# Twenty-four expert blocks computed ahead of the loop instead of sixteen, a loop period of eight steps, and the final sum joined to the last step

## The chip, the cores and the metric

The kernel runs on one core of one Trainium2 chip. The metric is the device time of one execution in microseconds (us), here the median of three. The core's engines run side by side, each through its own list of instructions, and wait for one another on semaphores: PE (TensorE, matrix multiplication; its accumulators are eight PSUM banks), DVE (VectorE), ACT (ScalarE), POOL (GpSimd, which here issues the indirect gathers) and SP (SyncE, which issues most DMA transfers).

## What is computed

One decoder layer over 1,024 tokens of width 1,024 in float32, then a final RMSNorm. Its first half (attention and a gated MLP) is untouched by the change. The second half is a PEER layer: a retrieval over 128 x 128 single-neuron experts with eight heads and sixteen picks per head.

```python
def peer(h, w_query, sub_keys, expert_u, expert_v):
    q = (hf @ w_query).reshape(n, PEER_HEADS, 2, PEER_HALF)
    scores = jnp.einsum('nhpd,hpkd->nhpk', q, sub_keys)
    s_top, i_top = lax.top_k(scores, PEER_TOPK)
    ...
    gates = jax.nn.softmax(best_s, axis=-1)
    u, vv = jnp.take(expert_u, idx, axis=0), jnp.take(expert_v, idx, axis=0)
    act = jax.nn.gelu(jnp.einsum('thkd,td->thk', u, h))
    return jnp.einsum('thk,thkd->td', gates * act, vv)
...
h2 = modulate(rmsnorm(x, norm2_g), sh2, sc2)
x = x + g2 * peer(h2, w_query, sub_keys, expert_u, expert_v)
return rmsnorm(x, final_g)
```

## The kernel before

Of the 1,024 tokens 640 (`DENSE`) go densely over all 16,384 experts: their gates are scattered into a table of weights, and 64 loop steps take two blocks of 128 experts each. The other 384 tokens (`GATHERED`, three tiles of 128) get their picked rows of `expert_u` and `expert_v` by indirect DMA and are worked row by row on DVE.

The second half has four stages.

**Retrieval** (`retrieve`). For each head a "chunk" on PE: query matmuls (`ring.unit`, L195, in groups of matmuls 128x512), scores (L1441). DVE searches the top sixteen and combines, ACT copies and computes exponentials (`exponentials`, L1491 and L1494) and part of the one-hot products (`one_hot`, L1502 and L1504), POOL the rest of the decoding. After the last chunk comes the tail: PE transposes the rows of the gathered tokens (`h_rows`, six groups, L1471), ACT copies them out (L1550), DVE ranks the last head, decodes it and normalises. A barrier closes the stage.

**Blocks ahead** (`Ahead`). Sixteen of the 128 blocks of the dense first layer (u times h, then gelu) are computed before the loop and kept in DRAM: four inside chunks 4 to 7 of retrieval, twelve inside the scatter. One block takes a `turn` on PE (eight transposes, L1267), `upper` on ACT (the high part, L1293), `leave` on PE (takes the high part off, L1275), `lower` on ACT (the low part, L1300), two `hide` units on PE (24 matmuls 128x320 each, L1285), two gelus on ACT (L1307, another function table than the exponentials'), and two stores by SP.

**Scatter** (`Scatter`): the weight table, with twelve blocks in between.

**The loop** (`experts`). At step j PE runs the `hide` units of step j + 1 (L2038, four for two blocks) and ten `share` groups of six matmuls 128x512 of the second layer (L2045), between them the `turn` units of step j + 2 (four transposes each, L2030). Four share groups stay in banks 4 to 7 for the whole loop; six are added into `acc` by DVE (`add`, L2267), and their banks are taken from a queue of four that also serves hide and turn. In every fourth step (j = 3) one of the two blocks comes from DRAM (`load_pre`), so it has two hide and two turn units instead of four: a short step. DVE also makes the low parts (L2211, L2216), the products with the weights (L2250, L2256) and the work of the six rows of a step (`row_dot` L2221, `row_add` L2234). The order of all this is written out by hand; nothing plans it.

The end of the loop and the sum behind it are two blocks with a barrier between them:

```python
            add(NI, PERIOD - 2, False)
            split_v(NSTEP - 1)
            for k in range(3):
                row_add(NSTEP - 1, 3 + k)
            add(NI, PERIOD - 1, False, True)
```

`finish` then loads the gate row, the residual x and the last gain, and per tile of 128 tokens multiplies (three of eight on POOL), adds, and norms (DVE L2359 to L2379), tile 0 first.

## Time and profile before

| | |
|---|---|
| device time, median of 3 runs | 3261.34 us (3261.26 to 3266.68) |
| profiled execution: time, span | 3260.53 us, 3258.8 us |
| mean granted clock of TensorE | 0.974 of full |
| busy: PE, PE weight load | 3041.0 us (93%), 2696.0 us (83%) |
| busy: DVE, ACT, POOL | 2574.8 us (79%), 1102.8 us (34%), 1267.2 us (39%) |
| DMA queues: POOL's gathers, SP's transfers | 35.9% and 31.2% of 16 engines' span |

All times inside the program are counted from the start of the span, which is 1.7 us shorter than the execution's own time. Retrieval's chunks 2 to 7 run from 911.6 to 1117.7 us, its tail to 1163.5, the loop fills most of the rest, and the last 40 us are the final sum. "Granted clock" is the share of TensorE's full clock that the chip gave in a stretch.

### The profile page before, as it was taken

To read this page: it belongs to the slowest core of one execution; us is meant where nothing else is said; L and a number is where in the kernel's file an instruction comes from. 1 tells how busy PE (TensorE), PEld (TensorE's weight loads), DVE (VectorE), ACT (ScalarE), POOL (GpSimd) and SP (SyncE) were. 2 spreads that over 40 slices of the span, in tenths; PEclk is the share of its full clock that TensorE was granted. 3 is DMA by queue.
4 is the path that set the end of the run, shared out by engine and by line. 5 is a ranking of instruction groups with operands and counts; after the bars stand their busy time and mean duration, and the time that the engine had idled before them with its cause. 6 is when DMAs were issued, how large, how long until landed. Compare 5 with 4: busy or idle time off the path is not lost. (4 is left out here: it accounts for less than half of the span.)

```text
span 3258.8 us, 53120 instructions
## 1 busy us (share of the span) xinstructions
PE 3041.0 (93%) x18277; PEld 2696.0 (83%) x18277; DVE 2574.8 (79%) x5156; ACT 1102.8 (34%) x2027; POOL 1267.2 (39%) x969
## 2 busy tenths in 40 slices
PE   6999999999789869889999999999999999999993
PEld 4998888779678768778888889888888888898883
DVE  5455333474489989879999999999999999999997
ACT  3222666503345536522222222222222222222222
POOL 0001000010167700045555555555555555555552
PEclk9999999999899989999999999999999999999997
DMA  6435333143301028889899889888998988989885
GB/s 237 152 128 179 107 104 104 72 138 115 103 16 47 9 95 272 264 324 326 312 321 324 317 313 328 318 313 322 317 321 312 331 313 319 318 314 322 315 305 194
DMA packets 331871, 760.99 MB, mean 234 GB/s; under 512 B 20348, under 2 KB 171480, under 8 KB 331744
## 3 DMA queue, kind: packets, MB, share of 16 engines
q0 software_dynamic: 115712, 419.48, 35.9%
q1 hardware_dynamic: 214976, 335.65, 31.2%
q10 hardware_dynamic: 1056, 4.19, 0.3%
q8 instruction: 75, 1.23, 0.2%
q14 instruction: 52, 0.43, 0.0%
HBM read 686.86 MB, written 72.39 MB: 233 GB/s over the span
## 5 line engine op out<-in xcount | busy, mean ns | idle before, releaser
L1987 POOL DMA_INDIRECT ex_u_row<-in_expert_u,ex_row x384 | 487.7, 1270 | 687.1 <-DVE ex_dot L2221 405.4
L1987 POOL DMA_INDIRECT ex_v_row<-in_expert_v,ex_row x384 | 530.3, 1381 | 333.1 <-DVE acc L2234 262.3
L2234 DVE SCALAR_TENSOR_TENSOR acc<-ex_v_row,ex_coef,acc 128x1024 f32<-128x1024 f32 x384 | 491.4, 1280 | 14.7 <-issue 2.3
L2221 DVE CUSTOM_DVE_ANT_0 ex_u_row<-ex_u_row,h_rows 128x1024 f32<-128x1024 f32 x384 | 467.1, 1216 | 1.8 <-DMA ex_u_row<-in_expert_u,ex_row 1.5
L2045 PE MATMUL psum<-ex_v_hi,ex_c_lo 128*128 128x512 f32 x1280 | 423.0, 412 | 39.7 <-DVE acc L2267 26.6
L2045 PE MATMUL psum<-ex_v_lo,ex_c_hi 128*128 128x512 f32 x1280 | 400.6, 394 | 0.0
L2045 PE MATMUL psum<-ex_v_hi,ex_c_hi 128*128 128x512 f32 x1280 | 397.0, 391 | 0.0
L2267 DVE TENSOR_TENSOR acc<-psum,acc 128x512 f32<-128x512 f32 x384 | 263.6, 686 | 57.0 <-PE psum L2045 46.4
L2038 PE MATMUL psum<-h_hi,h_lo 128*128 128x320 f32 x1792 | 300.1, 310 | 3.6 <-DVE h_lo L2211 3.6
L2038 PE MATMUL psum<-h_lo,h_hi 128*128 128x320 f32 x1792 | 299.5, 309 | 0.0
L2038 PE MATMUL psum<-h_hi 128*128 128x320 f32 x1792 | 299.2, 309 | 0.0
L2045 PEld LDWEIGHTS psum<-ex_v_lo,ex_c_hi 128*128 128x128 f32 x1280 | 241.3, 189 | 55.9
L2045 PEld LDWEIGHTS psum<-ex_v_hi,ex_c_hi 128*128 128x128 f32 x1280 | 241.0, 188 | 55.8
L2045 PEld LDWEIGHTS psum<-ex_v_hi,ex_c_lo 128*128 128x128 f32 x1280 | 219.9, 189 | 80.6 <-DVE acc L2267 37.8
L2038 PEld LDWEIGHTS psum<-h_hi,h_lo 128*128 128x128 f32 x1792 | 275.1, 188 | 9.0 <-issue 4.2
L2038 PEld LDWEIGHTS psum<-h_lo,h_hi 128*128 128x128 f32 x1792 | 272.4, 188 | 0.0
L2038 PEld LDWEIGHTS psum<-h_hi 128*128 128x128 f32 x1792 | 272.0, 188 | 0.0
L2147 ACT ACTIVATE ex_c_hi<-ex_g 128x320 fp32r<-128x320 f32 x222 | 104.8, 472 | 425.9 <-DVE ex_g L2250 424.4
L2126 ACT ACTIVATE ex_v_hi<-ex_vn 128x2048 fp32r<-128x2048 f32 x64 | 122.8, 1918 | 310.7 <-PE psum L2045 310.7
L2120 ACT ACTIVATE h_hi<-psum 128x512 fp32r<-128x512 f32 x224 | 129.4, 593 | 274.1 <-PE psum L2030 265.5
L2211 DVE TENSOR_TENSOR h_lo<-psum,h_hi 128x512 fp32r<-128x512 f32 x224 | 152.5, 682 | 23.1 <-ACT h_hi L2120 22.8
L2216 DVE TENSOR_TENSOR ex_v_lo<-ex_vn,ex_v_hi 128x2048 fp32r<-128x2048 f32 x64 | 146.7, 2292 | 11.4 <-issue 9.9
(338 smaller groups left out, 5324.8 us busy)
## 6 DMA issues: line engine op xcount, KB each, us to landing
ex_vn<-in_expert_v SPq DMA_DIRECT2D x64, 1024.0 KB
ex_un<-in_expert_u SPq DMA_DIRECT2D x48, 1024.0 KB
w_dram<-sc_w SPq DMA_DIRECT2D x10, 4096.0 KB, 14.9
ex_w<-w_dram SPq DMA_DIRECT2D x64, 640.0 KB
gm_wm<-in_w_mod SPq DMA_DIRECT2D x16, 1024.0 KB, 5.1
pj_raw<-in_w_in SPq DMA_DIRECT2D x11, 1024.0 KB, 7.5
qk_dram<-pj_staged_r POOLq DMA_DIRECT2D x32, 256.0 KB, 3.2
gt_raw<-in_w_in SPq DMA_DIRECT2D x16, 512.0 KB, 4.0
```

The lines of the kernel that those rows point to most:

```text
L1987: nc.gpsimd.indirect_dma_start(to[:], None, all_rows, bass.IndirectOffsetOnAxis(row[s][:, col:col + 1], 0)).then_inc(done, 16)
L2038: last = nc.tensor.matmul(core.bank[bank][:, 0:HD], lhsT, rhs, start=m == 0, stop=m == len(ops) - 1)
L2045: last = nc.tensor.matmul(out, lhsT, rhs, start=m == 0 and not kept, stop=m == len(ops) - 1, skip_group_check=kept)
L2120: nc.scalar.activation(ut(h.hi, q // 2, (q % 2) * 4, 4), core.bank[banks[q]].rearrange("p (k n) -> p k n", k=4), ACT.Copy).then_inc(u_hi, 1)
L2126: nc.scalar.activation(vh.hi[:], vn[:], ACT.Copy).then_inc(v_hi, 1)
L2147: nc.scalar.activation(ch[s].hi[:, e, half * HD:(half + 1) * HD], x, ACT.Copy).then_inc(c_hi, 1)
L2211: nc.vector.tensor_tensor(ut(h.lo, q // 2, (q % 2) * 4, 4), core.bank[bank].rearrange("p (k n) -> p k n", k=4), ut(h.hi, q // 2, (q % 2) * ...
L2216: nc.vector.tensor_tensor(vh.lo[:], vn[:], vh.hi[:].bitcast(F32), ALU.subtract).then_inc(v_lo, 1)
L2221: nc.vector.tensor_tensor_reduce(out=u_row[k % 3][:], in0=u_row[k % 3][:], in1=h_rows[:, k % 3, :], scale=1.0, scalar=0.0, op0=ALU.mult, o ...
L2234: nc.vector.scalar_tensor_tensor(out=to, in0=v_row[k % 3][:], scalar=coef[:, k:k + 1], in1=to, op0=ALU.mult, op1=ALU.add).then_inc(row_use ...
L2267: nc.vector.tensor_tensor(to, core.bank[SHARE_BANKS[j][n] if turning else LAST_SHARE_BANKS[j][n]], to, ALU.add).then_inc(added, 1)
```

## The change

Twenty-four blocks are ahead instead of sixteen. `HEADS` goes from four to six: chunks 2 to 7 of retrieval each hold one block (`FIRST_JOB` 4 becomes 2). `TAIL`, new, puts six blocks (6 to 11) into retrieval's tail, behind the transposes of `h_rows` on PE, each `hide` with the next block's turn or leave ahead of it; on ACT the tail's exponentials and one-hot products are put between the blocks' copies and gelus. The scatter keeps twelve. The loop's period is eight steps, of which 2, 5 and 7 are short. At its end the last step's `expert_v` is split ahead of the adds into a part of `h` that is no longer read, while the step before still reads `vh`, and `finish` becomes a class `Finish` whose lists are the tail of the loop's own lists: no barrier, its loads go out once the last hide unit is done, the tiles go in the order 5, 6, 7, 2, 3, 4, 0, 1, the six last adds stand inside its totals, and all eight multiplications are on DVE.

```diff
-    HEADS = 4
-    BLOCKS = NKEYS // 8
+    HEADS, TAIL = 6, 6
+    SHORT, PERIOD = (2, 5, 7), 8
+    BLOCKS = NKEYS // 2 // PERIOD * len(SHORT)
...
+    def place_tail(self):
+
+        at, bank = self.core.at, self.core.bank
+        self.tail = Site([at(f"ah_un_ta{m}", 4 * m, [P, D])[:] for m in range(2)],
+                         [at(f"ah_g_ta{m}", 8 + 1.25 * m, [P, HD])[:] for m in range(2)],
+                         [at(f"ah_hi_ta{m}", 16 + 4 * m, [P, KD, P], F32R)[:] for m in range(2)],
+                         [at(f"ah_lo_ta{m}", 64 + 4 * m, [P, KD, P], F32R)[:] for m in range(2)], bank[0:2], bank[2:4])
...
+    def site(self, n):
+
+        return self.heads if n < self.HEADS else self.tail if n < self.HEADS + self.TAIL else self.scatter
+
+    def row(self, n):
+
+        return n // len(self.SHORT) * 2 * self.PERIOD + 2 * self.SHORT[n % len(self.SHORT)] + 1
...
     def load(self, sp, n, m):
         sp.wait_ge(self.turned, n * 2 + 2)
-        sp.dma_start(self.un[m][:], self.u_rows[:, bass.ds(n * 8 + 7, 1), :].rearrange("j a d -> j (a d)")).then_inc(self.un_in[m], 16)
+        sp.dma_start(self.site(n).un[m], self.u_rows[:, self.row(n), :]).then_inc(self.un_in[m], 16)
...
-        if n < self.HEADS:
+        if n <= self.HEADS:
             pe.wait_ge(self.gelued, n * 2 + 2)
...
-    JOBS, FIRST_JOB = ahead.HEADS, 4
+    JOBS, TAIL_END, FIRST_JOB = ahead.HEADS, ahead.HEADS + ahead.TAIL, 2
...
-            for n in range(JOBS):
-                if n + 2 < JOBS:
+            query_weights(4)
+            for n in range(TAIL_END):
+                if n + 2 == JOBS:
+                    sp.wait_ge(ring.hi_done[0], NPAIR + 1)
+                    sp.wait_ge(ring.lo_done[0], NPAIR + 1)
+                if n + 2 < TAIL_END:
                     ahead.load(sp, n + 2, n % 2)
+                if n + 5 < PH:
+                    query_weights(n + 5)
                 for half in range(2):
                     ahead.store(sp, n, half)
             for half in range(2):
-                sp.wait_ge(ahead.stored[half], JOBS * 16)
+                sp.wait_ge(ahead.stored[half], TAIL_END * 16)
...
+            ahead.turn(pe, JOBS, JOBS % 2, JOBS // 2)
+            ahead.leave(pe, JOBS, JOBS % 2)
+            for n in range(JOBS, TAIL_END):
+                for half in range(2):
+                    m = n + 1
+                    if m < TAIL_END and half == 0:
+                        ahead.turn(pe, m, m % 2, m // 2)
+                    if m < TAIL_END and half == 1:
+                        ahead.leave(pe, m, m % 2)
+                    ahead.hide(pe, n, n % 2, half)
...
+            def block_in(n):
+                ahead.upper(act, n, n % 2)
+                ahead.lower(act, n, n % 2)
+
+            def block_out(n):
+                for half in range(2):
+                    ahead.gelu(act, n, half)
+
             for n in range(2 * GATHERED):
                 act.wait_ge(h_turned, n + 1)
                 nc.scalar.activation(h_rows[:, n // 2, (n % 2) * HALF:(n % 2 + 1) * HALF], core.bank[4 + n % 2], ACT.Copy).then_inc(h_copied, 1)
+            block_in(JOBS)
+            block_in(JOBS + 1)
+            exponentials(PH - 2)
+            block_out(JOBS)
+            block_in(JOBS + 2)
+            one_hot(PH - 2)
+            block_out(JOBS + 1)
+            block_in(JOBS + 3)
+            block_out(JOBS + 2)
+            block_in(JOBS + 4)
+            block_out(JOBS + 3)
             exponentials(PH - 1)
+            block_in(JOBS + 5)
+            block_out(JOBS + 4)
+            block_out(JOBS + 5)
...
+    PERIOD, SHORT = ahead.PERIOD, ahead.SHORT
+    LAGGING = [j - 1 for j in SHORT]
+    PER = 4 * PERIOD - 2 * len(SHORT)
...
-        return 2 if j % PERIOD == PERIOD - 1 else 4
+        return 2 if j % PERIOD in SHORT else 4
 
     def before(i, j, n):
 
 
-        return i * PER + (j // PERIOD * PER + 4 * (j % PERIOD) + n)
+        return i * PER + (j // PERIOD * PER + sum(units(k) for k in range(j % PERIOD)) + n)
...
-    def load_pre(sp, i):
-        sp.wait_ge(c_lo, i * (4 * PERIOD) + PRIME)
-        sp.dma_start(pre[:], ahead.dram[bass.ds(i, 1)].rearrange("a e h t -> e (a h) t")).then_inc(pre_in, 16)
+    def load_pre(sp, i, j):
+        k = SHORT.index(j)
+        sp.wait_ge(c_lo, i * (4 * PERIOD) + (4 * (j - 1) + PRIME))
+        sp.dma_start(pre[:], ahead.dram[bass.ds(i * len(SHORT) + k, 1)].rearrange("a e h t -> e (a h) t")).then_inc(pre_in, 16)
 
     NI = NSTEP // PERIOD - 1
+    ALL_HIDDEN = before(NI, PERIOD - 1, units(PERIOD - 1)) + PRIME
...
-                if j == 1:
-                    load_pre(sp, i)
+                if j + 2 in SHORT:
+                    load_pre(sp, i, j + 2)
                 load_v(sp, c + 1)
 
...
             load_v(sp, NSTEP - 1)
+            sp.wait_ge(hidden, ALL_HIDDEN)
+            end.sync(sp)
...
+            def split_last_v():
+
+                act.wait_ge(vn_in, NSTEP * 16)
+                act.wait_ge(hidden, ALL_HIDDEN)
+                nc.scalar.activation(h.hi[:, 0:2, :], vn[:], ACT.Copy).then_inc(v_hi, 1)
...
-                if j == LAGGING and turning:
+                if j in LAGGING and turning:
                     split_u(i, j + 2, TURN_BANKS[j], range(2))
                     gelu_dots(c + 1, 0)
                     split_u(i, j + 2, TURN_BANKS[j], range(2, 4))
                 else:
+                    if last and j == PERIOD - 2:
+                        split_last_v()
                     if not final:
                         gelu_dots(c + 1, 0)
                     if turning:
                         split_u(i, j + 2, TURN_BANKS[j])
-                if j < PERIOD - 1 or turning:
+                if not last or j < PERIOD - 2:
                     split_v(c + 1)
                 if not final:
...
+                        dve.wait_ge(pre_in, i * (16 * len(SHORT)) + 16 * (SHORT.index(j) + 1))
                     nc.vector.tensor_tensor(x, x, w[s][:, half * NB // 2:(half + 1) * NB // 2, e * t.WB:(e + 1) * t.WB],
                                             ALU.mult).then_inc(weighed, 1)
-                    rows = 2 if j % PERIOD == LAGGING + 1 else 3
+                    rows = 2 if j % PERIOD in SHORT else 3
...
-                    if j != LAGGING or n >= 2:
-                        k = n - 2 if j == LAGGING else n
+                    if j not in LAGGING or n >= 2:
...
+            dve.wait_ge(v_hi, NSTEP + PRIME)
+            nc.vector.tensor_tensor(h.lo[:, 0:2, :], vn[:], h.hi[:, 0:2, :].bitcast(F32), ALU.subtract).then_inc(v_lo, 1)
             add(NI, PERIOD - 2, False)
-            split_v(NSTEP - 1)
             for k in range(3):
                 row_add(NSTEP - 1, 3 + k)
-            add(NI, PERIOD - 1, False, True)
...
+    ORDER = (5, 6, 7, 2, 3, 4, 0, 1)
+    LOADS = (0, 2, 3, 5, 6, 8)
+    ADDS = {0: (0, 1), 1: (2,), 2: (3, 4), 3: (5,)}
...
+        sp.dma_start(self.g2[:], self.t.gate_rows[1:2, :].to_broadcast([P, D])).then_inc(self.g_in[0], 16)
+        for load, (k, end) in enumerate(zip(self.LOADS, self.LOADS[1:])):
+            c, n = self.ORDER[k], end - k
+            src = self.t.x2_dram[c * P:(c + n) * P, :]
+            sp.dma_start(self.x(k, n), src if n == 1 else src.rearrange("(t p) d -> p t d", p=P)).then_inc(self.x_in[load], 16)
+        sp.dma_start(self.fg[:], self.final_g.rearrange("(a d) -> a d", a=1).to_broadcast([P, D])).then_inc(self.g_in[1], 16)
+        for k, c in enumerate(self.ORDER):
+            sp.wait_ge(self.normed, k + 1)
+            sp.dma_start(self.out[0, c * P:(c + 1) * P, :], self.x(k)).then_inc(self.stored, 16)
+        sp.wait_ge(self.stored, TT * 16)
+
+    def vector(self, dve, add_last):
+
+        nc, acc = self.nc, self.acc
+
+        def total(k):
+
+            c = self.ORDER[k]
+            moe = self.core.psum[:, 4 + 2 * c:6 + 2 * c, :].rearrange("p b n -> p (b n)") if c < 2 else acc[:, c, :]
+            nc.vector.tensor_tensor(acc[:, c, :], moe, self.g2[:], ALU.mult)
+            for n in self.ADDS.get(k, ()):
+                add_last(n)
+            dve.drain()
+            dve.wait_ge(self.x_in[max(n for n, at in enumerate(self.LOADS) if at <= k)], 16)
+            nc.vector.tensor_tensor(self.x(k), self.x(k), acc[:, c, :], ALU.add).then_inc(self.summed, 1)
...
+        dve.wait_ge(self.g_in[0], 16)
+        for k in range(TT + 3):
+            if k < TT:
+                total(k)
+            if 2 <= k < TT + 2:
+                average(k - 2)
+            if k >= 3:
+                norm(k - 3)
...
-        experts(nc, core, t, expert_u, expert_v, h2, h_rows, acc, g_row, g_gate, ahead, scatter)
-        finish(nc, core, t, final_g, acc, out)
+        end = Finish(nc, core, t, final_g, acc, out)
+        experts(nc, core, t, expert_u, expert_v, h2, h_rows, acc, g_row, g_gate, ahead, scatter, end)
```

Of ACT, in the tail of retrieval, before: `ah_g_rt` is the gelu of the fourth block's halves (the rows above this piece), L1491 and L1494 are the exponentials of the last head but one, L1502 and L1504 its one-hot products.

```order
L1491 ACTIVATE rt_lowest<-rt_best 128x8
L1494 ACT_TABLE_LOAD
L1494 ACTIVATE pick_8579,rt_esum<-rt_best,rt_lowest 128x16 x8
L1502 ACTIVATE rt_hots<-rt_hots 128x2048
L1504 ACTIVATE rt_hots<-rt_hots 128x2048
L1502 ACTIVATE rt_hots<-rt_hots 128x2048
L1504 ACTIVATE rt_hots<-rt_hots 128x2048
L1550 ACTIVATE h_rows<-psum 128x512 x6
L1491 ACTIVATE rt_lowest<-rt_best 128x8
L1494 ACTIVATE pick_8579,rt_esum<-rt_best,rt_lowest 128x16 x8
```

After, from the copies of `h_rows` on (L1601 is that copy; L1323 is `upper`, L1330 `lower`, L1337 the gelu, L1536 and L1539 the exponentials; `ah_..._ta` are the tail's buffers):

```order
L1601 ACTIVATE h_rows<-psum 128x512 x6
L1323 ACTIVATE ah_hi_ta_8590<-psum 128x512 x2
L1330 ACTIVATE ah_lo_ta_8592<-psum 128x512 x2
L1323 ACTIVATE ah_hi_ta_8591<-psum 128x512 x2
L1330 ACTIVATE ah_lo_ta_8593<-psum 128x512 x2
L1536 ACTIVATE rt_lowest<-rt_best 128x8
L1539 ACT_TABLE_LOAD
L1539 ACTIVATE pick_8579,rt_esum<-rt_best,rt_lowest 128x16 x8
L1337 ACT_TABLE_LOAD
L1337 ACTIVATE ah_g_ta_8588<-psum 128x320
L1337 ACTIVATE ah_g_ta_8589<-psum 128x320
L1323 ACTIVATE ah_hi_ta_8590<-psum 128x512 x2
```

The copies of `h_rows` stand ahead of the exponentials now, and behind those come the gelus of block 6, with a load of their function table; the one-hot products follow block 8's copies.

Of PE in the same place: before, the transposes of `h_rows` (L1471) are its last work of the stage.

```order
L1471 MATMUL psum<-ident,h_lo 128x128
L1471 MATMUL psum<-ident,h_hi 128x128
L1471 MATMUL psum<-ident,h_lo 128x128
L1471 MATMUL psum<-ident,h_hi 128x128
L1352 UNCONDITIONAL_BRANCH
```

After (L1506 is the same transpose, L1297 `turn`, L1305 `leave`, L1315 `hide`):

```order
L1506 MATMUL psum<-ident,h_hi 128x128
L1297 MATMUL psum<-ident,ah_un_ta_8586 128x128 x8
L1305 MATMUL psum<-ah_hi_ta_8590,minus 128x512 x2
L1297 MATMUL psum<-ident,ah_un_ta_8587 128x128 x8
L1315 MATMUL psum<-h_hi,ah_lo_ta_8592 128x320 x8
L1315 MATMUL psum<-h_lo,ah_hi_ta_8590 128x320 x8
L1315 MATMUL psum<-h_hi,ah_hi_ta_8590 128x320 x8
L1305 MATMUL psum<-ah_hi_ta_8591,minus 128x512 x2
L1315 MATMUL psum<-h_hi,ah_lo_ta_8592 128x320 x8
L1315 MATMUL psum<-h_lo,ah_hi_ta_8590 128x320 x8
L1315 MATMUL psum<-h_hi,ah_hi_ta_8590 128x320 x8
L1297 MATMUL psum<-ident,ah_un_ta_8586 128x128 x8
```

Behind the last transpose stand twelve hide units, six turns and six leaves that weren't there.

Of DVE at the end of the loop, before: L2216 is the low part of the last step's `expert_v`, L2234 the last rows, L2267 the six last adds, L2359 and L2367 the first tile of the sum.

```order
L2216 TENSOR_TENSOR ex_v_lo<-ex_vn,ex_v_hi 128x2048
L2230 TENSOR_TENSOR ex_coef<-ex_act_dot,g_gate 128x3
L2234 SCALAR_TENSOR_TENSOR acc<-ex_v_row_12122,ex_coef,acc 128x1024
L2234 SCALAR_TENSOR_TENSOR acc<-ex_v_row_12123,ex_coef,acc 128x1024
L2234 SCALAR_TENSOR_TENSOR acc<-ex_v_row_12124,ex_coef,acc 128x1024
L2267 TENSOR_TENSOR acc<-psum,acc 128x512 x6
L1954 UNCONDITIONAL_BRANCH
L2352 UNCONDITIONAL_BRANCH
L2359 TENSOR_TENSOR acc<-psum,fi_g_18561 128x1024
L2367 TENSOR_TENSOR fi_xs<-fi_xs,acc 128x1024
```

After (L2312 is the row, L2401 a last add, L2449 the multiplication with the gate row, L2454 the addition of x):

```order
L2312 SCALAR_TENSOR_TENSOR acc<-ex_v_row_12855,ex_coef,acc 128x1024
L2312 SCALAR_TENSOR_TENSOR acc<-ex_v_row_12856,ex_coef,acc 128x1024
L2312 SCALAR_TENSOR_TENSOR acc<-ex_v_row_12857,ex_coef,acc 128x1024
L2449 TENSOR_TENSOR acc<-acc,fi_g_12833 128x1024
L2401 TENSOR_TENSOR acc<-psum,acc 128x512 x2
L2454 TENSOR_TENSOR fi_xs_12831<-fi_xs_12831,acc 128x1024
L2449 TENSOR_TENSOR acc<-acc,fi_g_12833 128x1024
L2401 TENSOR_TENSOR acc<-psum,acc 128x512
L2454 TENSOR_TENSOR fi_xs_12831<-fi_xs_12831,acc 128x1024
L2449 TENSOR_TENSOR acc<-acc,fi_g_12833 128x1024
```

The split has gone further up, ahead of step 62's adds, the branches of the barrier are gone, and the adds stand between the multiplication and the addition of tiles 5, 6, 7 and 2.

## Rows read from the trace of the kernel before

**Rows 1.** Windows in retrieval: us, busy PE, PEld, DVE, ACT, POOL, PEclk, DMA share, GB/s

```profile
911.60:942.80 31.20, 26.20 (x131) 21.51 (x129) 29.32 (x197) 19.48 (x41) 20.03 (x6) 1.00 0.00 1
...
975.70:1013.30 37.60, 36.89 (x185) 31.80 (x186) 36.45 (x202) 17.26 (x30) 28.56 (x19) 0.92 0.09 30
1082.80:1117.70 34.90, 34.19 (x190) 29.90 (x188) 32.81 (x203) 19.95 (x38) 25.03 (x22) 1.00 0.03 10
1117.70:1163.50 45.80, 13.77 (x98) 13.38 (x96) 42.72 (x222) 20.01 (x49) 18.43 (x10) 0.66 0.02 8
...
1112.38:1115.90 3.52, 3.52 (x25) 3.51 (x24) 3.26 (x10) 0.60 (x1) 2.40 (x4) 1.00 0.00 0
```

**Rows 2.** Windows in the loop: 1,600 us of it, and its four kinds of step

```profile
1500.00:3100.00 1600.00, 1577.04 (x8973) 1413.96 (x8972) 1477.71 (x2184) 426.28 (x851) 903.43 (x683) 1.00 0.90 319
2014.49:2043.19 28.70, 28.70 (x166) 26.12 (x164) 25.30 (x38) 6.94 (x14) 16.65 (x13) 1.00 0.93 331
2043.19:2067.74 24.55, 22.91 (x126) 19.78 (x125) 22.74 (x36) 7.25 (x14) 11.64 (x9) 1.00 0.84 284
2067.74:2097.68 29.94, 29.94 (x173) 26.84 (x172) 28.75 (x44) 7.70 (x16) 18.40 (x14) 1.00 0.92 332
2097.68:2127.36 29.68, 29.68 (x173) 26.91 (x172) 27.38 (x41) 8.20 (x16) 17.33 (x13) 1.00 0.91 323
```

**Rows 3.** Waits from 1500 to 3100 us: total, times, longest

```profile
PE psum L2045 <- DVE acc L2267: 22.9, 14, 1.6
```

**Rows 4.** Timeline of PE at one turn unit of the loop: start, us, operation, count

```profile
2051.61 0.60 PE L2030 MATMUL psum<-ident,ex_un 128*128 128x128 f32 x4
2051.97 0.71 PE L2045 MATMUL psum<-ex_v_hi,ex_c_lo 128*128 128x512 f32 x2
```

**Rows 5.** Timeline of PE in retrieval

```profile
1053.64 1.03 PE L1267 MATMUL psum<-ident,ah_un_rt 128*128 128x128 f32 x8
1054.43 2.07 PE L195 MATMUL psum<-h_hi,rt_w_lo 128*128 128x512 f32 x8
...
1062.65 0.70 PE L1275 MATMUL psum<-ah_hi,minus 128*128 128x512 f32 x2
...
1121.09 0.39 PE L1471 MATMUL psum<-ident,h_hi 128*128 128x128 f32 x2
```

**Rows 6.** Timeline of ACT in retrieval

```profile
1057.46 1.09 ACT L1293 ACTIVATE ah_hi<-psum 128x512 fp32r<-128x512 f32 x2 [0.24 <-issue]
...
1118.50 1.28 ACT L1307 ACT_TABLE_LOAD   x1
...
1120.44 0.22 ACT L1491 ACTIVATE rt_lowest<-rt_best 128x8 f32<-128x8 f32 x1
...
1125.23 1.91 ACT L1502 ACTIVATE rt_hots<-rt_hots 128x2048 bf16<-128x2048 bf16 x1 [0.79 <-POOL rt_hots L1406]
...
1132.81 1.06 ACT L1550 ACTIVATE h_rows<-psum 128x512 f32<-128x512 f32 x2
...
1147.16 0.21 ACT L1491 ACTIVATE rt_lowest<-rt_best 128x8 f32<-128x8 f32 x1 [3.09 <-DVEq L1600]
```

**Rows 7.** Timeline of PE and DVE at the end

```profile
3202.71 1.19 PE L2045 MATMUL psum<-ex_v_hi,ex_c_lo 128*128 128x512 f32 x2 [10.00 <-DVE ex_v_lo L2216]
...
3206.68 1.28 DVE L2234 SCALAR_TENSOR_TENSOR acc<-ex_v_row,ex_coef,acc 128x1024 f32<-128x1024 f32 x1 [1.60 <-DMA ex_v_row<-in_expert_v,ex_row]
...
3218.78 0.69 DVE L2267 TENSOR_TENSOR acc<-psum,acc 128x512 f32<-128x512 f32 x1 [0.67 <-PE psum L2045]
3224.06 1.22 DVE L2359 TENSOR_TENSOR acc<-psum,fi_g 128x1024 f32<-128x1024 f32 x1 [4.59 <-DMA fi_g<-gate_rows]
...
3233.05 1.21 DVE L2364 TENSOR_TENSOR acc<-acc,fi_g 128x1024 f32<-128x1024 f32 x1
...
3235.55 1.22 DVE L2367 TENSOR_TENSOR fi_xs<-fi_xs,acc 128x1024 f32<-128x1024 f32 x1
...
3254.49 1.28 DVE L2379 SCALAR_TENSOR_TENSOR fi_xs<-fi_xs,fi_s,fi_fg 128x1024 f32<-128x1024 f32 x1
```

More of the change, by code:

```diff
@@ L14 @@
 from contextlib import ExitStack
+from dataclasses import dataclass
 import concourse.bass as bass
@@ new lines, in place_scatter @@
+    def place_scatter(self):
+        at, bank = self.core.at, self.core.bank
+        columns = [slice(DENSE + m * P, DENSE + (m + 1) * P) for m in range(2)]
+        self.scatter = Site([at(f"ah_un_sc{m}", 180 + 4 * m, [P, D])[:] for m in range(2)],
+                            [at(f"ah_g_sc{m}", 197 + 1.25 * m, [P, HD])[:] for m in range(2)],
+                            [self.h.hi[:, :, c] for c in columns], [self.h.lo[:, :, c] for c in columns], bank[0:2], bank[2:4])
+    def site(self, n):
+        return self.heads if n < self.HEADS else self.tail if n < self.HEADS + self.TAIL else self.scatter
@@ L1413, in decode @@
                                             ALU.mult).then_inc(picked, 1)
-            for i in range(NPAIR - 1):
-                for s in range(2):
-                    ring.split_lo(nc.gpsimd, pool, s, i + 1, i * 2 * U + (s + 2) * U)
-                    decode(i * 2 + s, s)
-            decode(PH - 2, 0)
+            ring.split_lo(nc.gpsimd, pool, 0, 1, 2 * U)
+            for h in range(PH - 1):
+                decode(h, h % 2)
+                d = h + 3
+                if d < PH:
+                    ring.split_lo(nc.gpsimd, pool, d % 2, d // 2, d * U)
             core.clear_early(pool)
@@ L1756, in job @@
     def job(self, k):
-        n = self.ahead.HEADS + k
+        n = self.ahead.HEADS + self.ahead.TAIL + k
         return n, n % 2
@@ L1851, in stored_all, with experts @@
             eng.wait_ge(self.stored[s], self.TILES // 2 * 16)
-def experts(nc, core, t, expert_u, expert_v, h, h_rows, acc, g_row, g_gate, ahead, scatter):
+def experts(nc, core, t, expert_u, expert_v, h, h_rows, acc, g_row, g_gate, ahead, scatter, end):
     PRIME = 24
@@ L2039, in hide, with share @@
                 last.then_inc(hidden, 1)
-            def share(s, n, out, kept):
+            def share(s, n, out, kept, v):
                 tt, dh = n // 2, n % 2
-                ops = [(a[:, e, tt * P:(tt + 1) * P], b[:, e, dh * HALF:(dh + 1) * HALF]) for a, b in passes(ch[s], vh) for e in range(2)]
+                ops = [(a[:, e, tt * P:(tt + 1) * P], b[:, e, dh * HALF:(dh + 1) * HALF]) for a, b in passes(ch[s], v) for e in range(2)]
                 for m, (lhsT, rhs) in enumerate(ops):
@@ L2196, in _ @@
                 step(NI, j, j < PERIOD - 2, j == PERIOD - 1, True)
+            end.scalar(act)
         @block.vector
@@ L2259, in weigh, with add @@
                         row_add(adds, 3 + n)
-            def add(i, j, turning=True, last=False):
+            def add(i, j, turning=True):
                 c = i * PERIOD + j
@@ L2451, in decoder_layer @@
         ahead.place_heads()
+        ahead.place_tail()
         h_rows = core.at("h_rows", 128, [P, GATHERED, D])
```

173 lines of the change are left out of this document (70 added, 103 removed).

## Prediction

> **What bounds the kernel now.** I read the windows first. In 1,600 us of the loop PE is busy for 1577.04 [rows 2], so the loop is PE's; DVE, at 1477.71, stands close behind it, and the DMA engines are busy for 0.90. The waits of the same stretch say where PE's idle time is: 14 waits of up to 1.6 us on DVE's adds, which set banks free [rows 3]. The reader sees their place in the windows by step: a full period is 28.70 + 24.55 + 29.94 + 29.68 = 112.87 us, and only the 24.55 us piece, which holds the two hide units of the short step, has PE idle, 24.55 - 22.91 = 1.64 us [rows 2]. Retrieval's chunks are PE's when they hold a block (34.19 of 34.90 us) and DVE's when they don't (29.32 of 31.20, PE 26.20). In the tail PE works 13.77 of 45.80 us and DVE 42.72 [rows 1]: room for PE, and not for DVE. At the end PE waits 10.00 us for the last split, and from 3224.06 DVE runs the sum alone [rows 7].
>
> So every block ahead takes work off the bound of the loop, and puts it where PE is idle or where it isn't.
>
> **The loop.** A block ahead takes away two hide units and two turn units. A hide unit of 24 matmuls takes 3.52 us [rows 1]; a turn unit 2051.97 - 2051.61 = 0.36 [rows 4]. One block: 2 x 3.52 + 2 x 0.36 = 7.76; eight more: **-62.1**. Each short step also brings the stall of 1.64: 8 x 1.64 = **+13.1**, together -49.0. The same from the windows: call the piece of 28.70 A (its turns are the short step's two), the one of 24.55 B, the full ones C. Eight steps with shorts at 2, 5 and 7 run A B C A B A B C: 3 x 28.70 + 3 x 24.55 + 2 x 29.81 = 219.4 against 2 x 112.87 = 225.7, that is -6.3 a period, eight times -51. I take -49.
>
> Does DVE keep up? It does 25.30 + 22.74 + 28.75 + 27.38 = 104.17 us a period, 26.04 a step [rows 2]. In B it gets 22.74 done, 3.3 less than a mean step, and it catches up in the two pieces behind (28.75 and 27.38, above the mean). Now one B is followed by a single A before the next B. DVE's own work in A is 25.30 of 28.70, a room of 3.4 for those 3.3. It just fits. If it doesn't, each period pays up to 3.3 more at the third short step, 8 x 3.3 = 26: bounds of the loop -62 (the stalls vanish) and -23. The mean over a period fits in any case: 2 x 104.17 us of DVE in 219.4. The transfers stay the same bytes in less time, 319 x 225.7 / 219.4 = 328 GB/s; single pieces run at 331 to 332 [rows 2] without a wait of PE, so I cost them at nothing. Their cover is two steps of lead for each load.
>
> **Retrieval's heads.** Chunks 2 and 3 take 975.70 - 911.60 = 64.1 us without a block; with one each takes a chunk's 34.8 (chunks 5 to 7, from 1013.30 to 1117.70, are 104.4). That is +5.5. Chunk 4 took 37.60 at a granted clock of 0.92, behind two chunks in which PE waited; chunk 7 took 34.90 at 1.00 [rows 1]. With PE busy from chunk 2 on I expect 34.8 for it: -2.8. Heads: **+2.7** (bounds +2 and +5.5, if the dip stays). Chunk 7 then ends at 1120.4. DVE needs 32.81 of 34.90 there, so it isn't late.
>
> **Retrieval's tail.** It took 45.80. Now, on PE, from 1120.4:
> - the six groups of `h_rows`: two were done by 1121.48, 3.78 after the chunk's end [rows 5], six 11.3, now without the 12 us behind exponentials and one-hots, whose copies come first on ACT;
> - block 6's turn, high copies, leave, low copies: 1054.43 - 1053.64 = 0.79 [rows 5], 1.09 [rows 6], 0.5 (from the 0.70 of the leave, whose end overlaps), 1.09 again, and 0.4 of handing over: 3.9. Block 7's turn is inside it;
> - twelve hide units of 3.52: 42.2; four more turns of 0.79: 3.2; five leaves of 0.46 to 0.5: 2.4;
> - PE's waits on ACT. The exponentials take 4.0 (from 1120.44 to the one-hot's start at 1125.23, less its wait of 0.79), a table load 1.28, the one-hot products 1132.81 - 1125.23 = 7.6 [rows 6]. Block 7's first hide waits for block 6's first gelu, which stands behind exponentials and a table load: block 6's two hides, a turn and a leave give 8.3 us of cover, ACT needs about 10.9 (low copies, exponentials, load, gelu): 2.6. Block 8's waits for block 7's gelu behind low copies of 8 and the one-hots: 4.9. Block 11's leave and hides behind the last exponentials: 1.2. Sum 8.7;
> - last gelu, its store and the end of the stage: 3.2.
>
> That is 74.9. I add 2.8 for the clock: the tail before was at 0.66 with PE idle [rows 1], and after the two long waits I expect one dip like chunk 4's. 77.7 - 45.8 = **+31.9**. DVE is not the bound: it ended 16.4 us after the last exponentials were released at 1147.16 [rows 6], and is set back by the later exponentials and one-hots by some 20 us, to about 1184, where PE's work reaches to 1198. POOL (18.43 busy) has room too. SP's queue carries the loads two blocks ahead and both stores of a block behind them; a load is issued once the turn two blocks back is done, some 8 us ahead of its use. Bounds: no wait and no dip +20; waits twice as long and two dips +43.
>
> ACT now changes its function table three times on this path. Rows: the load takes 1.28, and two gelus lie right behind, 1118.50 + 1.28 + 0.66 = 1120.44 [rows 6]; that is what the sum uses. The Trainium skill (page "ScalarE: Activation LUTs", section "What ACT_TABLE_LOAD costs") adds to the load's 1.28 a drain of 1.38 in the pipeline, 2.66 us a switch. By the page the estimate would be 3 x 1.38 = 4.1 us more, 3240. The row shows no such gap in front of a gelu, so the row decides.
>
> **The end.** Before, the last row ended at 3207.96, the last add at 3219.47, the sum began at 3224.06 and its last norm ended at 3255.77, 3.0 ahead of the end of the span [rows 7]. Now the split stands ahead, PE has nothing to wait for but the step before, and DVE is the bound from the last row on. Its loads (4 MB of x, two rows spread to 0.5 MB each) go out beside the last gathers, of which the last row already waited 1.60: I allow 2.2, 3210.2. From there: a multiplication and an addition 3235.55 - 3233.05 = 2.5; an add 0.69; a norm 1.28 and about 0.2. Three totals with five adds 7.5 + 3.5, five with a norm and one add 20.0 + 0.7, three norms 4.5: 36.2, then 3.0: 3249.4 against 3258.8. POOL's three multiplications, which DVE takes over, are in it. **-9.4**, I take -9.5 (bounds -4, if the loads hold up the gathers, and -12).
>
> **Sum.** 3260.5 - 49.0 + 2.7 + 31.9 - 9.5 = 3236.6, from the profiled execution (3260.53). The median of the runs is 0.8 higher; I say **3236**.
>
> **The rivals.**
> - The tail costs nothing but its work: no waits (the gelus' order is caught by the eight microseconds of cover), no dip: 3236 - 11.5 = 3225. For it: chunk 7 has no wait. Against it: one-hots of 7.6 us in a single piece. 0.12.
> - DVE doesn't catch up between the two close short steps: +26, 3262, no change. For it: 3.3 against a room of 3.4. Against it: B's adds come early in the period, and most of the backlog is rows, which nobody on PE waits for. 0.13.
> - The joined sum brings nothing, as its loads delay the last gathers and the last `expert_v`: 3236 + 8 = 3244. For it: the wait of 1.60 on a gather [rows 7], and busy engines (0.90). 0.12.
> - Slower: in the tail PE's many short waits leave TensorE at the lower of its two levels, 1.2 GHz, throughout. The tail before was granted 0.66, and in it PE idled twice. Its 61 us of work take twice as long where clock bounds them: twelve hides 42 us more, 3278. It decides once the tail costs more than about 25 over my value. Against it: chunk 4 at 0.92 with only short idling ahead. 0.05.
> - The page's rule on table switches, 3240: 0.03, inside my own range.
> - The change does less than it says (blocks stored late, `load_pre` late behind SP's waits, so short steps wait for DRAM): 24 waits of 1 to 2 us, 3236 + 36 = 3272 at worst. Loads of 0.3 MB two steps ahead speak against it. 0.02.
>
> **How the numbers follow.** The forecast has 0.50, with a range of its own of 3228 to 3245. The rivals above 3254 have 0.20 together, but the second of them partly lands below, since only part of the backlog may stay; those below 3220 have next to nothing. So **3220 to 3254**. Within 0.2% (6.5 us, about what a measurement here can tell from no change) of 3261.3 is 3254.8 to 3267.9. Faster: forecast, no-wait tail, lost end, the page's rule, part of the backlog rival and the rest, 0.85; same 0.08; slower 0.07.
>
> **What would show it.** In the profile after: chunks 2 to 7 of 34.8 us each at a clock of 1.00; a tail of 78 us with PE busy some 60, its longest waits on the gelus behind the exponentials and one-hots; windows of eight steps of 219 us, PE's waits on the adds 3 in each, of 1.6 us; PE's wait ahead of the last shares gone; the last norm 3 us ahead of the end, 36 us behind the last row. Wrong would be: waits of 3 us and more on the adds in every period, a clock of 0.5 through the tail, or a last row later than 3215 (less what the rest gained).

## The result, and the profile after

The changed kernel takes 3275.76 us (median of five, 3273.09 to 3280.58) against 3261.34 (five, 3260.85 to 3266.68): ratio 1.0045, 95% interval 1.0034 to 1.0057. The change made the kernel slower by 0.45%. The forecast was 3236, and 3220 to 3254 as its range.

The windows of the changed kernel (columns as in rows 1) show the tail of retrieval, the scatter, chunk 7, and the loop:

```profile
1120.20:1196.50 76.30, 65.64 (x446) 63.19 (x446) 50.54 (x223) 41.05 (x88) 20.31 (x11) 0.96 0.18 59
1196.50:1417.50 221.00, 195.62 (x2017) 183.17 (x2017) 195.22 (x173) 121.00 (x240) 4.44 (x4) 0.95 0.74 229
1085.29:1120.13 34.84, 34.13 (x189) 29.83 (x188) 32.74 (x203) 19.92 (x37) 24.97 (x22) 1.00 0.08 25
1500.00:3100.00 1600.00, 1542.65 (x8612) 1370.75 (x8613) 1472.23 (x2183) 411.89 (x827) 936.15 (x684) 0.99 0.91 320
```

Retrieval ends at 1196.5, where the forecast had 1198, and before it was 1163.5 [rows 1]. The scatter takes 221.0 (219.5 before, from 1163.5 to 1383.0, where the loop's first hide unit starts). From the last step's hide units to the end there are 77.4 us, 86.9 before. So retrieval is +33.0, the scatter +1.5 and the end -9.5: all near the forecast. What is left of the 13.1 us between the spans (3271.9 and 3258.8) is the loop: -11.9 us, where the forecast had -49. **37 us are missing, all in the loop.** PE is busy there for 1542.65 of 1,600 us, where it was for 1577.04 [rows 2]: it waits more.

One period of eight steps of the changed kernel, and its last three pieces (columns as above):

```profile
2132.36:2357.32 224.96, 216.84 (x1208) 192.45 (x1209) 206.28 (x307) 57.57 (x117) 131.53 (x96) 0.99 0.90 320
...
2270.43:2299.40 28.97, 28.97 (x165) 26.05 (x164) 27.77 (x42) 6.51 (x14) 19.41 (x14) 1.00 0.94 341
2299.40:2326.14 26.74, 24.48 (x125) 21.00 (x124) 24.68 (x38) 7.25 (x14) 14.33 (x12) 0.94 0.89 314
2326.14:2357.32 31.18, 29.84 (x173) 26.72 (x172) 29.76 (x46) 9.12 (x17) 19.88 (x15) 1.00 0.94 334
```

The period takes 225 us and not 219.4. The second of the two short steps that are one apart costs 26.74 where B had 24.55 [rows 2], with the clock at 0.94, and the piece behind it 31.18 instead of 29.8.

The waits of the changed kernel in the same 1,600 us as in rows 3 (total, times, longest):

```profile
PE psum L2114 <- DVE acc L2345: 48.1, 28, 2.4
...
DVE acc L2345 <- issue: 33.3, 43, 4.6
...
PE psum L2107 <- issue: 5.4, 4, 1.6
...
PE psum L2107 <- DVE acc L2345: 4.3, 2, 2.7
```

PE waits twice as much for DVE's adds. And DVE stood still before its adds for up to 4.6 us without anything that the profile shows having held it; before, this entry read 9.0 us in 42 times, 0.2 at most. The timeline of DVE (start, us, operation) has the place:

```profile
2148.24 0.49 DVE L2334 TENSOR_TENSOR ex_c_lo<-ex_g,ex_c_hi 128x320 fp32r<-128x320 f32 x1 [0.54 <-ACT ex_c_hi L2222]
2152.86 0.69 DVE L2345 TENSOR_TENSOR acc<-psum,acc 128x512 f32<-128x512 f32 x1 [4.13 <-issue]
```

Between these two rows stands the branch at the end of DVE's loop body. It happens once a period, and only there. In the kernel before, the second of the same pair started 0.48 us behind the first, and here 4.62. The DMA queues of the stretch show what goes on beside it: two queues of kind "instruction", which before moved 1 and 2 packets in 1,600 us, and now

```profile
q8 instruction: 79, 1.29, 0.3%
q14 instruction: 42, 0.34, 0.1%
```

(queue, kind, packets, MB, share). DVE's body was 266 instructions long, by the count of its records between two branches, and is 526 now, since it holds eight steps.

The last two waits above, six in number and 9.7 us together, have no counterpart before. They are PE's, ahead of the first hide unit (L2107) of a new period, and there PE's own loop branches. The profile's view of that line (duration in ns, least, middle and most; first and last start) from 1,380 to 3,000 us shows what the branch takes, before and after:

```profile
L2100 PEldq COMPARE_BRANCH  x14: 207/208/235, 1529.7 to 2997.0; - x14
...
L2169 PEldq COMPARE_BRANCH  x6: 4807/5034/6097, 1674.1 to 2802.1; - x6
```

PE's body has 1,327 records of matmuls, weight loads and sequencer instructions before, and some 2,535 now. When the branch starts PE still has 3.7 to 4.2 us of matmuls in hand, so of the 4.8 to 6.1 us of a branch it idles for 1.0 to 2.7; the next matmul starts 0.36 or 0.37 us behind the branch's end, six times out of six. So both engines stand still at their branches. That the view names DVE's adds for two of PE's six waits doesn't contradict it: an add happened to end near by.

### The profile page after: what moved, and what is told of

It is laid out like the page before. It is cut to its first block, busy times and chain, and to the rows that moved or that the text cites. A ratio compares the mean times of both kernels' runs of the same rounds, so it can differ in the third digit from the quotient of the medians.

```text
span 3271.9 us, 52895 instructions
## 1 busy us (share of the span) xinstructions
PE 3059.9 (94%) x18293; PEld 2705.5 (83%) x18293; DVE 2571.6 (79%) x5143; ACT 1114.1 (34%) x2049; POOL 1289.8 (39%) x966
## 4 chain that ended last, share of the span: by engine, by line
PE 25%; DVE 19%; issue 8%; PEld 5%; DVEq 4%; DMA 1%; ACT 1%; PEldq 0%; ACTq 0%; POOLq 0%; SPq 0%
PE psum L2114 13%; PE psum L2107 11%; DVE acc L2312 5%; DVE ex_u_row L2299 4%; DVE acc L2345 3%; PEld psum L1315 3%; PEld psum L1859 2%; DVE ex_g L2328 2%; DVEq L2302 1%; DVE ex_c_lo L2334 1%; PE psum L2099 1%; DVEq L2309 1%; ACT ex_c_hi L2222 1%; DVE h_lo L2289 1%; DVE ex_pre L2328 1%
## 5 line engine op out<-in xcount | busy, mean ns | idle before, releaser
L2056 POOL DMA_INDIRECT ex_u_row<-in_expert_u,ex_row x384 | 506.3, 1318 | 703.8 <-DVE ex_dot L2299 410.2
L2056 POOL DMA_INDIRECT ex_v_row<-in_expert_v,ex_row x384 | 540.1, 1406 | 281.0 <-DVE acc L2312 201.7
L2312 DVE SCALAR_TENSOR_TENSOR acc<-ex_v_row,ex_coef,acc 128x1024 f32<-128x1024 f32 x384 | 491.9, 1281 | 17.4 <-DMA ex_v_row<-in_expert_v,ex_row 4.1
L2107 PE MATMUL psum<-h_hi,h_lo 128*128 128x320 f32 x1664 | 279.6, 310 | 13.9 <-issue 5.4
L2107 PE MATMUL psum<-h_lo,h_hi 128*128 128x320 f32 x1664 | 280.0, 311 | 0.0
L2107 PE MATMUL psum<-h_hi 128*128 128x320 f32 x1664 | 278.8, 310 | 0.0
L2107 PEld LDWEIGHTS psum<-h_hi,h_lo 128*128 128x128 f32 x1664 | 255.3, 188 | 21.4 <-issue 11.9
L2107 PEld LDWEIGHTS psum<-h_lo,h_hi 128*128 128x128 f32 x1664 | 254.8, 189 | 0.0
L2107 PEld LDWEIGHTS psum<-h_hi 128*128 128x128 f32 x1664 | 253.8, 189 | 0.0
L2189 ACT ACTIVATE h_hi<-psum 128x512 fp32r<-128x512 f32 x208 | 118.6, 592 | 189.3 <-PE psum L2099 189.3
L2289 DVE TENSOR_TENSOR h_lo<-psum,h_hi 128x512 fp32r<-128x512 f32 x208 | 141.6, 682 | 14.2 <-ACT h_hi L2189 14.2
```

What stands on the lines that cost most here:

```text
L2056: nc.gpsimd.indirect_dma_start(to[:], None, all_rows, bass.IndirectOffsetOnAxis(row[s][:, col:col + 1], 0)).then_inc(done, 16)
L2107: last = nc.tensor.matmul(core.bank[bank][:, 0:HD], lhsT, rhs, start=m == 0, stop=m == len(ops) - 1)
L2189: nc.scalar.activation(ut(h.hi, q // 2, (q % 2) * 4, 4), core.bank[banks[q]].rearrange("p (k n) -> p k n", k=4), ACT.Copy).then_inc(u_hi, 1)
L2289: nc.vector.tensor_tensor(ut(h.lo, q // 2, (q % 2) * 4, 4), core.bank[bank].rearrange("p (k n) -> p k n", k=4), ut(h.hi, q // 2, (q % 2) * ...
L2312: nc.vector.scalar_tensor_tensor(out=to, in0=v_row[k % 3][:], scalar=coef[:, k:k + 1], in1=to, op0=ALU.mult, op1=ALU.add).then_inc(row_use ...
```

## Experiments

**1. DVE's loop written out, and two controls.** The edit of the first, to the changed kernel:

```diff
-            with dve.Fori(0, NI) as i:
+            for i in range(NI):
                 for j in range(PERIOD):
                     step(i, j)
```

> The changed kernel, with DVE's loop alone written out in full (no branch, waits on constants); all other engines keep their loops. Theory A (DVE's loop of eight steps is 526 instructions long, and at each taken branch DVE stands still for 4.2 to 4.9 us, with transfers of the instruction queues beside it, where the loop of 266 took 0.27): the standstills go, and with them most of the 37 us by which the loop missed the forecast: 3240 to 3250 us. Theory B (the two short steps one apart leave DVE behind, the branch costs nothing by itself): 3272 to 3276, with the waits on the adds where they were.

Measured: 3254.17 us (ten runs, 3248.02 to 3260.1), ratio to the kernel before 0.9977 (0.9966 to 0.9987): faster than theory B allows, but 4 us above the range of theory A. The same edit on the kernel before:

> Control for the first: the kernel before with DVE's loop written out. Theory A: its branch cost 0.27 us, so only the register instructions go, and DVE is not the bound: 3255 to 3262 us. If writing DVE out gives 20 us and more here too, the first run's gain is no proof of the standstill.

Measured: 3258.76 (3256.0 to 3261.55), ratio 0.9986 (0.9977 to 0.9996), against 3263.04 for the kernel before on this chip: 4 us. So of the 21.6 us that the first run gained on the changed kernel, some 17 are not the register instructions (a written-out loop waits on constants and needs none). DVE's standstills are gone from the waits, and the loop is 32.9 us shorter than before instead of 11.9. The forecast's -49 is still 16 away: theory A holds, but not for all of it. PE's loop was left as it is in this run, and so were its standstills: six branches of 4.6 to 5.8 us, and PE idle for 8.4 us behind them. The seventh period ends at a branch that is not taken: there PE doesn't wait, and with its clock at full speed too that period takes 219.7 us, where 219.4 was forecast.

The other way round, the kernel before with a longer body and the same work:

```diff
-            with dve.Fori(0, NI) as i:
-                for j in range(PERIOD):
-                    step(i, j)
+            with dve.Fori(0, NI // 2) as pair:
+                for k in range(2):
+                    for j in range(PERIOD):
+                        step(pair * 2 + k, j)
+            for j in range(PERIOD):
+                step(NI - 1, j)
```

> The kernel before (sixteen blocks, period of four) with nothing changed but the form of DVE's loop: two periods to an iteration, some 530 instructions, seven iterations. Theory A: the standstill of 4 to 5 us appears at each of six taken branches, PE pays 2 to 5 us for each: 3261 + 12 to 30 = 3273 to 3291 us. Theory B: no change, 3258 to 3264, since the work and its order are the same.

Measured: 3277.84 (3275.75 to 3279.92), ratio 1.0047 (1.003 to 1.0064). The body is 530 instructions long, and DVE's timeline in that run shows the gap at the branch:

```profile
2123.05 0.49 DVE L2256 TENSOR_TENSOR ex_c_lo<-ex_g,ex_c_hi 128x320 fp32r<-128x320 f32 x1 [0.54 <-ACT ex_c_hi L2147]
2128.44 0.69 DVE L2267 TENSOR_TENSOR acc<-psum,acc 128x512 f32<-128x512 f32 x1 [4.90 <-issue]
```

Sixteen blocks, a period of four, no change of work or order, and 15 us lost: 227.2 to 229.8 us for eight steps where the kernel before has 225.7. That is theory A without the rest of the change. The queues tell the engines apart: here q14 has 40 packets and q8 two, so q14 feeds DVE and q8 PE. PE's body is as before in this run, and its branch takes 0.21 us, while DVE stands still for 3.9 to 5.2; in the first run, where DVE has no branch, PE's takes 4.6 to 5.8.

**2. The joined sum alone** (`HEADS` 4, `TAIL` 0, `SHORT` (3,), `PERIOD` 4, and the tail's lists as before):

```diff
-    HEADS, TAIL = 6, 6
-    SHORT, PERIOD = (2, 5, 7), 8
+    HEADS, TAIL = 4, 0
+    SHORT, PERIOD = (3,), 4
...
```

> The joined final sum alone, with sixteen blocks and the period of four, all else as in the kernel before. The forecast's term for the end was -9.5 us: 3251 to 3253 us. If the end's gain came from the rest of the change (an earlier last step), it would be 3259 to 3261.

Measured: 3252.83 (3251.39 to 3256.49), ratio 0.9973 (0.9962 to 0.9983): -10.2 us against the -9.5 of the forecast's term.

**3. Where the short steps stand.** Two short steps in eight, with DVE written out; the two kernels differ in one number:

```diff
-    SHORT, PERIOD = (2, 5, 7), 8
+    SHORT, PERIOD = (5, 7), 8
```

> DVE written out as in the first run, with two short steps in eight, 5 and 7, so sixteen blocks (six in the heads, six in the tail, four in the scatter). What the first run left open is 2.8 us a period above 219.4, all of it in the last two of its eight pieces. Theory C (two short steps one apart leave DVE behind; PE's wait there is above 2 us instead of 1.6, and the granted clock falls to 0.94 in that piece): the piece ahead of step 7 takes 26.6 us and the one behind it 30.6 to 31, the period 228 to 229 us. Theory D (three short steps in eight are too many for DVE or the DMA engines in the mean, wherever they stand): with two in eight nothing of it is left, 225.4 to 226.0.

> The same with the short steps 2 and 5, two full steps between them. Theories C and D: 225.4 to 226.0 us a period, no piece at a clock below 1.00, the waits on the adds 1.6 us each. If it shows 228 too, both fall, and it is the period of eight itself. The scatter with four blocks instead of twelve is shorter by 0 to 14 us (what DVE waits for PE there); the whole 3266 to 3280.

Measured, over six periods each: 227.5 to 229.3 us (mean 228.4) with 5 and 7; 225.1 to 226.8 (mean 225.8) with 2 and 5. The windows of a period with 5 and 7, and of the pieces ahead of step 7 and behind it:

```profile
2127.87:2356.98 229.11, 223.84 (x1264) 200.51 (x1265) 211.23 (x312) 61.28 (x121) 127.49 (x97) 0.99 0.89 318
...
2298.90:2325.51 26.61, 24.49 (x126) 21.01 (x124) 24.70 (x38) 7.25 (x14) 14.23 (x12) 0.94 0.88 314
2325.51:2356.98 31.47, 29.85 (x173) 26.73 (x172) 30.20 (x46) 9.41 (x17) 19.91 (x15) 1.00 0.94 341
```

and of a period with 2 and 5, and the piece of its second short step:

```profile
2125.24:2351.37 226.13, 222.42 (x1265) 199.13 (x1264) 209.37 (x310) 60.76 (x121) 125.58 (x97) 1.00 0.90 320
...
2236.80:2261.26 24.46, 22.92 (x126) 19.79 (x124) 22.88 (x36) 7.25 (x14) 11.55 (x9) 1.00 0.84 293
```

As many short steps, the same work, and 2.6 us a period more where only one full step lies between two of them. The traces put 1.6 of the 2.6 in the piece ahead of step 7 (26.1 in the mean, where the second short step of the other kernel takes 24.5), and 0.9 at PE's branch, whose idle time is 7.5 us over these periods with 5 and 7 and 2.0 with 2 and 5. Why the branch costs less there is open. Theory C holds for the first part, and D falls: with two in eight the loss in that piece is as large as with three. Where it arises is in PE's timeline of experiment 1, in the piece ahead of step 7:

```profile
2301.66 1.15 PE L2114 MATMUL psum<-ex_v_hi,ex_c_lo 128*128 128x512 f32 x2 [2.12 <-DVE acc L2345]
2302.61 1.05 PE L2114 MATMUL psum<-ex_v_lo,ex_c_hi 128*128 128x512 f32 x2
2303.47 1.05 PE L2114 MATMUL psum<-ex_v_hi,ex_c_hi 128*128 128x512 f32 x2
...
2305.65 0.62 PE L2114 MATMUL psum<-ex_v_lo,ex_c_hi 128*128 128x512 f32 x2
```

PE had waited 2.12 us for a bank, and for some 3.4 us behind that two matmuls take 1.05 instead of 0.62: TensorE runs at the lower of its levels (1.2 GHz; the piece's mean is 0.94), which costs PE another 24.49 - 22.91 = 1.6 us. The waits of 1.64 in the kernel before had no such trail: its 1,600 us stand at 1.00 [rows 2]. Not every pair does it: the wait of 2.1 us is there in all seven periods of experiment 1, the dip in four of them, and in the other three the piece took 25.0 at full clock. The loss in the next piece is another: it ends with PE's branch, and is longer than 29.69 by what PE idles there and some 0.2 us more. In the seventh period, with no branch taken, it takes 29.69.

These two runs took 3296.9 (5 and 7) and 3274.9 (2 and 5) as a whole; the second is inside its 3266 to 3280. They show besides what blocks in the scatter cost: with four instead of twelve the scatter of the first was 209.5 us long, 11.5 less than in the changed kernel and 8.3 less than in experiment 1's first run. DVE is busy for 194 to 195 us of it with four blocks as with twelve. So a block costs 1.0 to 1.4 us there, not the 7.8 that it saves in the loop.

**4. Two more heads, no tail.** Sixteen blocks as six, none and ten, with the joined sum and DVE written out; the edit is against experiment 2's kernel, and DVE's loop is left out of it:

```diff
-    HEADS, TAIL = 4, 0
+    HEADS, TAIL = 6, 0
```

> Sixteen blocks with the period of four, the joined sum and DVE written out, but six blocks in the heads, none in the tail and ten in the scatter. The joined sum gave 3253, DVE written out another 4, two more heads cost 2.7, and two blocks fewer in the scatter give 0 (DVE's bound) to 18 us (PE's): 3234 to 3252, I take 3246.

Measured: 3251.38 (3246.12 to 3253.52), ratio 0.9965 (0.9952 to 0.9977). Inside the range, at its slow end: the two blocks out of the scatter gave little (217.3 us for it, 219.4 before), as experiment 3 explains.

**5. The tail with four banks.** Experiment 1's kernel, DVE's loop written out; the lines that give odd blocks banks 4 and 5 are left out here:

```diff
...
     def hide(self, pe, n, m, half):
         pe.wait_ge(self.lo_out, n * 2 + 4)
-        pe.wait_ge(self.gelued, n * 2 + (half + 1))
+        early = 2 if self.HEADS < n < self.HEADS + self.TAIL else 0
+        pe.wait_ge(self.gelued, n * 2 + (half + 1) - early)
...
             block_in(JOBS + 2)
-            one_hot(PH - 2)
+            one_hot(PH - 2, [0])
             block_out(JOBS + 1)
             block_in(JOBS + 3)
+            one_hot(PH - 2, [1])
             block_out(JOBS + 2)
             block_in(JOBS + 4)
             block_out(JOBS + 3)
-            exponentials(PH - 1)
             block_in(JOBS + 5)
+            exponentials(PH - 1)
             block_out(JOBS + 4)
...
```

> The first run's kernel, with the tail's hide units in four banks instead of two (odd blocks in banks 4 and 5), the one-hot products in two parts with a gelu pair and a block's copies between them, and the last exponentials behind block 11's copies. If PE's 7.5 us of waits in the tail and the two clock dips behind them (1.6 and 1.4 us) are the gelus' order, they go: 3254 - 10 = 3242 to 3248. If ACT is the tail's bound, the waits come back elsewhere: 3251 to 3255.

Measured: 3241.59 (3238.91 to 3242.71), ratio 0.9941 (0.9924 to 0.9957), the fastest of all: 20 us under the kernel before, 34 under the changed one, and some 12 under experiment 1's, from which it differs by the tail alone; that is just under its own range. The window over its tail:

```profile
1120.20:1187.00 66.80, 63.46 (x458) 61.88 (x457) 52.01 (x226) 41.09 (x90) 20.62 (x12) 1.00 0.20 67
```

The tail ends at 1185.7, 10.8 us earlier, with no wait of 0.5 us or more ahead of its barrier, and at full clock. The banks, the one-hot products in two parts and the later exponentials went in together; what each gave is not told apart.

**6. From which length on the branch costs.** The kernel before, with drains that wait for nothing behind each step of DVE's loop (30, 46, 56 or 64):

```diff
                 for j in range(PERIOD):
                     step(i, j)
+                    for _ in range(30):
+                        dve.drain()
```

> The kernel before, its DVE loop made longer by 30 drains (which wait for nothing) behind each step: 266 + 4 x 30 = 386 instructions. It shows at which length of body the standstill at the taken branch begins, read at the branch itself; the drains cost DVE some 2 us a step, so the whole is slower by up to 60 us and its time says little. Theory A with the limit between 266 and 526 anywhere: 0.3 us at the branch if it lies above 386, 4 to 5 if below. If the standstill belonged to the period of eight or to the doubled work, none of the four shows it.

> The same with 46 drains a step, 450 instructions. 0.3 us at the branch if the limit is above, 4 to 5 if below; I expect 0.3.

> The same with 56 drains a step, 490 instructions. The Trainium skill (page on the runtime, section on instruction fetch) gives most engines room for 512 instructions; by that 0.3 us here, if the room is used to the last block, and 4 to 5 if part of it is spent on what comes next.

> The same with 64 drains a step, 522 instructions, as long as the changed kernel's loop of 526. Theory A: 4 to 5 us at each of 14 taken branches. If this shows 0.3, length is not the cause.

The times of one run each (3440.58, 3458.74, 3472.7, 3518.1 us) say little, since the drains load DVE: nearly 180 us for 30 a step is far above the 60 that I expected, partly by the standstills themselves (14 in each run, of 4.5 to 7.9 us). What counts is the time from DVE's taken branch to its next instruction, read at every taken branch but the first of each loop (behind 386 instructions or more that first one takes 3.9 to 7.8 us):

```text
body  kernel                        at a taken branch
266   before                        0.27 us
386   30 drains a step              6.0 to 7.9
450   46                            5.2 to 7.2
490   56                            4.5 to 7.2
522   64                            4.8 to 7.2
526   changed kernel                4.2 to 4.9
530   before, two periods a body    4.2 to 5.2
```

The limit lies between 266 and 386, lower than I expected (0.3 us at 450). DVE's timeline of the run with 386, whose gap holds 30 drains as well:

```profile
2063.00 0.49 DVE L2256 TENSOR_TENSOR ex_c_lo<-ex_g,ex_c_hi 128x320 fp32r<-128x320 f32 x1 [0.54 <-ACT ex_c_hi L2147]
2072.00 0.69 DVE L2267 TENSOR_TENSOR acc<-psum,acc 128x512 f32<-128x512 f32 x1 [8.51 <-issue]
```

It is the length, not the period of eight nor the work in it. And what DVE waits for is its own code. In all 68 standstills of these six traces a packet of DVE's instruction queue q14 lands within it, and DVE's next instruction starts 1.3 to 1.7 us behind that packet's end, however long the standstill was; at the 14 taken branches of the kernel before no such packet moves. PE's branches do the same: in the changed kernel and in the runs of experiments 1, 3 and 5 that kept its body of eight steps (30 taken branches in all), the branch ends 1.2 to 2.0 us behind a packet of q8. The Trainium skill (page "Runtime: NRT & Kernel Launch", section "Instruction fetch mechanics") says that a taken branch to code which is no longer in the engine's instruction memory waits for a DMA fetch; the runs agree. Its figure for the room, 512 instructions on engines other than PE, did not decide here: bodies of 386 to 490 stood still too.

## Why the prediction was wrong, point by point

- **The loop, -49: failed.** It was -11.9. The step that failed is the one from the windows of a step to eight steps in a row ("Eight steps with shorts at 2, 5 and 7 run A B C A B A B C"), with its check "Does DVE keep up?". Three costs were missing. The first wasn't in the forecast at all: DVE's body went from 266 to 526 instructions, and at each of six taken branches it stood still for 4.2 to 4.9 us. The working summed what PE and DVE do in a period, but DVE's list doesn't only grow by what it does. Writing DVE's loop out gave the loop 21 of the 37 us, 4 of them register instructions by the control.
- The second is the same cost on PE: its body doubled too, and its six taken branches left it idle for 9.7 us, 8.4 in the run with DVE written out. No run writes PE's loop out, so what that would give the whole is not measured.
- The third was there, in the sentence "It just fits": a backlog of 3.3 us against a room of 3.4. It didn't fit. With DVE written out the period is 221.8 in the mean of six where 219.4 was forecast; in the mean the piece ahead of step 7 is 1.4 us longer than the other short steps' pieces, and PE's branches take 1.1 a period. In the piece the wait of PE is 2.1 us instead of 1.6, and about 1.6 us of lower clock follow in four of seven periods, which the rival didn't have. Over seven periods that piece takes 9.7 us more than B seven times. Together with PE's 8.4 that is 18 of the 20 us that are to be explained (the 16 between -32.9 and -49, and the 4 of the register instructions). The rival (0.13) was right in its mechanism and too high in its price (3.3 a period). Its 3262, no change, was nearer than the forecast, but by luck: most of the loss came from the two branches, which it didn't have either.
- **A block's price, 7.76, and the stalls of 1.64: held**, where the steps stand apart. The pieces A, B and C in the middle of the changed kernel's period take 28.69, 24.56 and 30.01 us.
- **The heads, +2.7: held.** Chunks 2 to 7 took 208.6 us (six times 34.77) at a clock of 1.00, and chunk 4's dip went.
- **The tail, +31.9: held**, +30.5 by 76.3 us against 45.8. PE's waits were 2.28 and 4.53 where 2.6 and 4.9 were worked out; the clock fell behind both (a dip of 1.6 and one of 1.4, by hide units of 5.3 and 5.0 us instead of 3.7), 3.0 against 2.8. Each load of a function table took 1.28 us and the next operation followed at most 0.02 us behind it, as the row said; the 1.38 us more of the rival on table switches did not appear.
- **The end, -9.5: held**, -9.5, and -10.2 measured alone. The last row ended at 3233.6; the last rows waited up to 2.01 us for their gathers, where 2.2 was allowed.
- **The transfers: held.** DMA share 0.91 at 320 GB/s, no wait of PE on a load in the loop.
- **The range and the chances.** The range's slow end was made of the backlog alone. A body twice as long, on DVE and on PE, was a change that the diff showed in plain sight, and no case of the forecast had a price for it. The one case that went past the range on the slow side through the tail (0.05) had another mechanism: TensorE's clock was 0.96 there, and not at its lower level throughout. The chances named add up to 0.97.

What the change was for, blocks out of the loop, pays once DVE is written out and the tail has four banks: 24 blocks run at 3241.6 then, and sixteen with the joined sum and DVE written out at 3251.4. With DVE written out alone 24 blocks take 3254.2, and pay nothing against those. As it stood, the loop's gain of 11.9 us and the joined sum's of 9.5 were less than the 33.0 of retrieval.
